# Inverse norms by square root and reciprocal, and another order of work at three places, in a one-core network of three layers

## The reference, cut to what matters

```python
def rms_norm(x, gain):
    y = x * lax.rsqrt(jnp.mean(x * x, axis=-1, keepdims=True) + EPS)
    return y * gain
h = rms_norm(x, norm_mix[i]) * (1.0 + sc1) + sh1
x = x + g1 * mixer(h)
h = rms_norm(x, norm_ffn[i]) * (1.0 + sc2) + sh2
x = x + g2 * conv_ffn(h, ...)
```

## Time and profile before

| what | value |
|---|---|
| median of 3 runs | 1092.78 us (1092.67 to 1094.19) |
| the profiled execution's own time | 1092.73 us |
| its span, first to last instruction | 1091.0 us |
| outside the span | 1.7 us |
| TensorE clock granted, mean | 0.997 |
| busy: TensorE (PE), VectorE (DVE), ScalarE (ACT) | 98%, 74%, 31% |

### The profile page before, as it was taken

How to read it: one execution, slowest core, us unless ns; L and a number is a source line. 1 busy time by engine, 2 the same in 40 slices (tenths; PEclk the granted TensorE clock), 3 DMA queues, 4 the chain that set the end, 5 groups by cost and what they waited for, 6 DMA issues and landing times.

```text
span 1091.0 us, 18364 instructions
## 1 busy us (share of the span) xinstructions
PE 1069.7 (98%) x7516; PEld 972.7 (89%) x7516; DVE 808.4 (74%) x1392; ACT 337.6 (31%) x799; POOL 23.9 (2%) x83
## 2 busy tenths in 40 slices
PE   6999999999999999999999999999999999999998
PEld 4788889999999977888899999998898889999997
DVE  2477769888898848544789889887896298887755
ACT  3243324111111245663511111116355342222101
POOL 1000240000000000000000000000000000000000
PEclk9999999999999999999999999999999999999999
DMA  9999936888878662281868878775342255853421
GB/s 343 281 385 340 316 114 251 304 317 281 320 279 295 199 78 77 86 259 53 318 214 322 313 270 309 271 243 162 117 155 78 80 172 170 290 185 107 145 72 39
DMA packets 163013, 234.82 MB, mean 215 GB/s; under 512 B 8770, under 2 KB 137842, under 8 KB 162930
## 3 DMA queue, kind: packets, MB, share of 16 engines
q1 hardware_dynamic: 162428, 233.27, 63.5%
q10 hardware_dynamic: 501, 0.38, 0.1%
HBM read 232.19 MB, written 1.44 MB: 214 GB/s over the span
## 4 chain that ended last, share of the span: by engine, by line
PE 88%; DVE 7%; ACT 2%; issue 1%; DMA 1%; ACTq 1%; DVEq 0%
PE PS L869 34%; PE PS L915 13%; PE PS L799 11%; PE PS L827 6%; PE PS L990 6%; PE PS L812 4%; PE PS L1117 3%; PE PS L791 1%; PE PS L720 1%; PE PS L1475 1%; DVE scratch L2480 1%; PE PS L1321 1%; PE PS L1277 1%; DVE top L2479 1%; PE PS L1070 1%
## 5 line engine op out<-in xcount | busy, mean ns | idle before, releaser
L915 PE MATMUL PS<-act,slots 128*128 128x256 f32 x704 | 159.8, 380 | 0.4 <-DVE act L2191 0.4
L1962 DVE SCALAR_TENSOR_TENSOR ada_acc<-ada_slots,cond,ada_acc 128x1024 f32<-128x1024 f32 x119 | 152.6, 1282 | 5.1 <-DMA ada_slots<-in_ada_w 0.9
L1607 ACT ACTIVATE PS<-PS 128x128 f32<-128x128 f32 x180 | 53.5, 297 | 304.4 <-PE PS L869 304.4
L915 PEld LDWEIGHTS PS<-act,slots 128*128 128x128 f32 x704 | 130.5, 190 | 18.9 <-issue 1.6
L799 PE MATMUL PS<-hT,slots 128*128 128x256 f32 x656 | 144.3, 380 | 0.8 <-ACT hT L1569 0.8
L799 PEld LDWEIGHTS PS<-hT,slots 128*128 128x128 f32 x656 | 123.9, 190 | 19.2 <-issue 3.0
L869 PE MATMUL PS<-hT,slots 128*128 128x128 f32 x960 | 127.0, 275 | 0.0
L869 PE MATMUL PS<-oT,slots 128*128 128x128 f32 x960 | 126.8, 275 | 0.0
L869 PEld LDWEIGHTS PS<-hT,slots 128*128 128x128 f32 x960 | 119.6, 192 | 2.5
L869 PE MATMUL PS<-oT,scratch 128*128 128x128 f32 x960 | 117.1, 275 | 0.0
L869 PEld LDWEIGHTS PS<-oT,slots 128*128 128x128 f32 x960 | 116.8, 192 | 0.0
(11 more groups left out here) (403 smaller groups left out, 1405.4 us busy)
## 6 DMA issues: line engine op xcount, KB each, us to landing
ada_slots<-in_ada_w SPq DMA_DIRECT2D x144, 512.0 KB, 8.5
slots<-in_ffn_w_up SPq DMA_DIRECT2D x44, 1024.0 KB, 11.8
slots<-in_ffn_w_down SPq DMA_DIRECT2D x22, 1024.0 KB, 5.0
slots<-in_w_up SPq DMA_DIRECT2D x22, 1024.0 KB, 5.2
slots<-in_sb_w_in SPq DMA_DIRECT2D x11, 1024.0 KB, 13.1
slots<-in_w_in SPq DMA_DIRECT2D x11, 1024.0 KB, 5.4
slots<-in_dsa_w_in SPq DMA_DIRECT2D x10, 1024.0 KB, 5.3
ada_slots<-in_w_down SPq DMA_DIRECT2D x2, 2816.0 KB, 12.7
```

What stands on the lines that cost most here:

```text
L915: last = mm(PS[:, c // 2, (c % 2) * T:(c % 2) * T + T], w[:, j_odd * D + c * P:j_odd * D + (c + 1) * P], act[:, j_odd, :], start=start and ...
L1607: act_e.activation(dst.rearrange("p (x t) -> p x t", x=copies), stem(at).unsqueeze(1).to_broadcast([P, copies, P]), ACT.Copy).then_inc(see ...
L1962: ins = dve.scalar_tensor_tensor(dst, ada_slot[k][:, :], c, dst, ALU.mult, ALU.add)
```

## The change

It does four things.

1. Inverse roots. ScalarE's `root` and `norm_root` do one Sqrt (bias epsilon) where they did Ln and Exp, and VectorE does a RECIPROCAL in place behind it: on 128x256 for the six norms and for two of the other roots, on 128x1024 for the recurrence's. `norm_root` preloads the table of Sqrt in place of that of Ln; `norm_raw` preloads that of Silu behind it.
2. Second mixer. TensorE does the index products between and behind the projections of slot 5, and `values(1)` moves from in front of `index(2)` to behind `query_sums(1)`, in front of `turn_sums(1)`. ScalarE's `read_v(1)` goes behind `take_sums(1)`. VectorE's copy of the last projection goes between the second and third pair of heads.
3. Third mixer. `window_norm` stands in front of `decayed_halves(5)`, `decayed_near(6)` behind the two `block_collect`. On ScalarE the first gate stands in front of the second `window_probs`, the second behind the copies of levels 0 and 1; the tables of Silu and Sqrt are preloaded.
4. Last feed-forward stage. `weight_sums` has three parts where it had two halves: only its first sum stands in front of the update of the last chunks.

```diff
 # TensorE, second mixer
-            arrived(5)
-            fill(2)
-            project(4, 5, 0, hT, first_frees=4)
-            project(5, 5, 1, hT).then_inc(unit_full[2], 1)
...
             last.then_inc(unit_full[3], 1)
-            pe.wait_ge(lat_ready, 1)
-            values(0)
+            arrived(5)
+            fill(2)
+            project(4, 5, 0, hT, first_frees=4)
             index(0)
             index(1)
+            project(5, 5, 1, hT).then_inc(unit_full[2], 1)
+            pe.wait_ge(lat_ready, 1)
+            values(0, frees=5)
             pe.wait_ge(k_squared, 1)
             fill(2)
             mm(PS[:, 4, 0:T], ones[:, :], k_sq[:, :], start=True, stop=True).then_inc(unit_full[2], 1)
-            values(1)
             index(2)
             index(3)
...
             scores(0)
             turn_sums(0)
             query_sums(1)
+            values(1)
 # ScalarE
             def root(dst, ps):
                 full(2)
-                link(act_e.activation(dst, ps, ACT.Ln, bias=eps_col[:, :]))
-                act_e.activation(dst, dst, ACT.Exp, scale=-0.5).then_inc(unit_read[2], 1)
-            def norm_root(bank):
-                act_e.preload_act_table(ACT.Ln)
+                act_e.activation(dst, ps, ACT.Sqrt, bias=eps_col[:, :]).then_inc(unit_read[2], 1)
+            def norm_root(bank, load_table=True):
+                if load_table:
+                    act_e.preload_act_table(ACT.Sqrt)
                 act_e.wait_ge(stat_full, bk("stat_full").next())
-                link(act_e.activation(rstd[:, :], PS[:, bank, 0:T], ACT.Ln, bias=eps_col[:, :]))
-                act_e.activation(rstd[:, :], rstd[:, :], ACT.Exp, scale=-0.5).then_inc(rstd_ready, 1)
+                act_e.activation(rstd[:, :], PS[:, bank, 0:T], ACT.Sqrt, bias=eps_col[:, :]).then_inc(norm_root_ready, 1)
 # ScalarE, norm_raw
-                norm_root(0)
+                norm_root(0, load_table)
+                act_e.preload_act_table(ACT.Silu)
 # ScalarE, second mixer
-            read_v(0)
             read_index(0)
             read_index(1)
-            read_v(1)
+            read_v(0)
...
             query_roots(0)
             take_sums(1)
+            read_v(1)
             softmax(0)
 # ScalarE, third mixer
             window_scale()
+            act_e.preload_act_table(ACT.Silu)
+            block_gate(hg, GH0, 0, 0)
             window_probs()
-            block_gate(hg, GH0, 0, 0, 0)
-            block_gate(hg, GH0, 1, 1, 1)
+            skip(0)
+            skip(1)
             full(0)
             act_e.activation(cross, PS[:, 0, :], ACT.Copy).then_inc(unit_read[0], 1)
...
+            block_gate(hg, GH0, 1, 1)
             skip(2)
+            act_e.preload_act_table(ACT.Sqrt)
 # VectorE
+            def inverse_root():
+                dve.wait_ge(norm_root_ready, bk("norm_root_ready").next())
+                link(dve.reciprocal(rstd[:, :], rstd[:, :]))
 # norm() and normalise() call it in place of their wait; in the first norm:
             norm_parts(4)
+            inverse_root()
             dve.wait_ge(ada_used[KC - 1], 1)
...
-            dve.wait_ge(rstd_ready, bk("rstd_ready").next())
 # VectorE, second mixer
-            full(2)
-            dve.tensor_copy(fm[:, 3:5, :], PS[:, 4:6, 0:T]).then_inc(unit_read[2], 1)
...
             for pair in range(IH // 2):
+                if pair == 2:
+                    full(2)
+                    dve.tensor_copy(fm[:, 3:5, :], PS[:, 4:6, 0:T]).then_inc(unit_read[2], 1)
...
                 if n == 4:
                     root()
+                    link(dve.reciprocal(rstd[:, :], rstd[:, :]))
 # VectorE, third mixer
             block_w_sums(GH0 + SLAB, 1)
+            window_norm()
             decayed_halves(5)
-            decayed_near(6)
-            window_norm()
             for i in range(2):
                 block_collect(i, i)
                 dve.nop().then_inc(block_taken, 1)
+            decayed_near(6)
...
             take_scores(4, 1)
             dve.wait_ge(unit_read[2], rstd_taken)
+            link(dve.reciprocal(rstd[:, :], rstd[:, :]))
...
             root()
+            link(dve.reciprocal(sq_flat[:, D:2 * D], sq_flat[:, D:2 * D]))
 # VectorE, weight_sums(l, n, parts=(0, 1, 2)): part 0 is L2076, part 1 L2077, part 2 L2079 and L2080
-                    weight_sums(2, 0, (1,))
+                    weight_sums(2, 0, (1, 2))
```

More of the change, by code:

```diff
@@ L278, in build @@
         stat_full = sem("stat_full")
-        rstd_ready = sem("rstd_ready")
+        norm_root_ready = sem("norm_root_ready")
         gain_ready = sem("gain_ready")
@@ L1213, in _, with values @@
             project(3, 4, 1, hT).then_inc(unit_full[1], 1)
-            arrived(5)
-            fill(2)
-            project(4, 5, 0, hT, first_frees=4)
-            project(5, 5, 1, hT).then_inc(unit_full[2], 1)
-            def values(tt):
+            def values(tt, frees=None):
                 fill(0)
@@ L1223, in values @@
                     last = mm(PS[:, g, :], fm[:, 0, tt * P:(tt + 1) * P], uv_w[:, 8 * g:8 * g + 8, :], start=True, stop=True)
+                    if g == 0 and frees is not None:
+                        last.then_inc(slot_used[frees], 1)
                 last.then_inc(unit_full[0], 1)
@@ L1242, in _ @@
                                     ident[64:64 + IH, 64:64 + IH])
-                if tt == 0:
-                    last.then_inc(slot_used[5], 1)
             last.then_inc(unit_full[3], 1)
-            pe.wait_ge(lat_ready, 1)
-            values(0)
+            arrived(5)
+            fill(2)
+            project(4, 5, 0, hT, first_frees=4)
             index(0)
             index(1)
+            project(5, 5, 1, hT).then_inc(unit_full[2], 1)
+            pe.wait_ge(lat_ready, 1)
+            values(0, frees=5)
             pe.wait_ge(k_squared, 1)
@@ L1573, in squares, with norm_raw @@
                 act_e.activation(hT[:, c:c + k, :], xT[:, c:c + k, :], ACT.Square, scale=D ** -0.5).then_inc(sq_ready, 1)
-            def norm_raw(units):
+            def norm_raw(units, load_table=True):
                 act_e.wait_ge(gain_ready, bk("gain_ready").next())
@@ L1834, in window_scale, with block_gate @@
                     last.then_inc(p_ready, 1)
-            def block_gate(dst, name_at, u, i, buf):
-                skip(u)
+            def block_gate(dst, name_at, i, buf):
                 act_e.wait_ge(block_taken, i + 1)
@@ L1902, in _ @@
             root(sq_flat[:, D:2 * D].rearrange("p (b n) -> p b n", b=2), PS[:, 4:6, :])
-            norm_raw(OUT_UNITS[2])
+            norm_raw(OUT_UNITS[2], load_table=False)
             ffn(2)
@@ L2063, in out_projection, with weight_sums @@
                         after()
-            def weight_sums(l, n, halves=(0, 1)):
+            def weight_sums(l, n, parts=(0, 1, 2)):
                 g, v = LAST_SETS[(n + 1) % 3] if l == 2 else (3 - 3 * (n % 2), 4 - 3 * (n % 2))
                 gate, val, ws = slot[g], slot[v], w_sum[n % 2]
-                if 0 in halves:
+                if 0 in parts:
                     for s, landed in zip((g, v), up_landed[l, n + 1]):
@@ L2076, in weight_sums @@
                     link(dve.tensor_tensor(ws[:, 0, :, :], val[:, 0:HALF, :], val[:, HALF:KC, :], ALU.add))
+                if 1 in parts:
                     link(dve.tensor_tensor(val[:, 0:HALF, :], gate[:, 0:HALF, :], val[:, 0:HALF, :], ALU.subtract))
-                if 1 in halves:
+                if 2 in parts:
                     link(dve.tensor_tensor(ws[:, 1, :, :], ws[:, 0, :, :], gate[:, 0:HALF, :], ALU.subtract))
@@ L2237, in last_chunks @@
                         if not odd and n + 1 < 10:
-                            weight_sums(2, n + 1, (1,))
+                            weight_sums(2, n + 1, (2,))
                         elif odd and n + 2 < 10:
-                            weight_sums(2, n + 2, (0,))
+                            weight_sums(2, n + 2, (0, 1))
                         elif p == 17:
@@ L2300, in ffn @@
                         chunk(odd, odd, raw[:, odd, 0, :], raw[:, odd, 1, :])
-                    weight_sums(2, 1, (0,))
+                    weight_sums(2, 1, (0, 1))
                     for odd in range(2):
```

## The result

After the change the kernel takes 1100.79 us (median of 4 runs, 1100.01 to 1103.92); beside it the kernel before took 1092.72. The ratio is 1.0077 (95% interval 1.0064 to 1.0089): 8.1 us slower, where the prediction had +2.95 and a range that ended at 1099.5. The profiled execution took 1100.2, with a span of 1098.5 and a mean granted clock of 0.998.

The account below looks back on a forecast made before the run. TensorE, busy 98% of the span, was taken to bound the kernel, so only holes closing or opening count. Stalls behind reciprocals less the reorderings' gains summed to +2.95 us on 1092.73, 1095.7; the 8-in-10 range was 1088.6 to 1099.5.

Parts of the forecast that it names:

- The term of the reciprocal: VectorE's reciprocal priced at 4.8 ns an element: 1.39 us on 128x256 and 5.1 us on 128x1024.
- the first norm: First norm: the reciprocal runs ahead of the conditioning vector's sums, so TensorE starts later, +0.9 us.
- the two feed-forward stages: Norms before the first and second feed-forward stage: the reciprocal outlasts VectorE's 0.6 us of slack, +0.8 us each.
- attention: Attention's root, third mixer: the reciprocal exceeds VectorE's 0.2 us of slack, +1.2 us.
- the recurrence: Recurrence's root: the 128x1024 reciprocal delays `mixed_ready` to 862.8, past TensorE's cover until 860.3, +2.5 us.
- third rival: All the new reciprocals: 8.3 ns an element, 2.3 and 8.7 us, about 1105 us in total; chance 0.07.
- the likeliest case: Whole kernel: reciprocal at the slope of its two small sizes, range 1094 to 1100.6 us; chance 0.56.
- Second mixer: Second mixer's new order: earlier index products close holes, a new one of 0.9 to 1.2 opens at `read_v(1)`; -0.25 us.
- Third mixer: Third mixer's new order: load and first gates ahead of the second `window_probs` close TensorE's 1.7 and 0.26 us holes; -1.9 us.
- Rival 2: Hole at `read_v(1)` or late gates do not pay, 1.9 us gain shrinks to 1: 1096.7; chance within the likeliest's 0.56.
- Rival 1: All new reciprocals as fast as other VectorE work, 0.43 and 1.23 us: 1089.1 us, faster; chance 0.27.
- Rival 4: ScalarE's roots: the table load stays because another function comes between preload and Sqrt, costing 1.3 us at two norms; chance 0.02.

Follow-up runs that it names:

- experiment 6: The kernel before with six unused reciprocals on 4 to 512 elements, one behind the other, in VectorE's second mixer: 1094.46 us, a single run.
- experiment 5: The kernel after, with TensorE making 9 products that nobody reads while it waits for `mixed_ready`: 1099.15 us, ratio 1.0058 to the kernel before.
- experiment 2: The kernel before with all inverse roots by Sqrt and reciprocal, the orders as they were: 1108.53 us, ratio 1.0138.
- experiment 12: The kernel before, no order changed, with the table set holding both Ln and Exp preloaded by name and Silu's behind: 1091.41 us, ratio 0.9986.
- experiment 7: The kernel before with only the second mixer's new order, roots by Ln and Exp: 1092.55 us, ratio 0.9999 to the kernel before.
- experiments 9: The kernel after with Ln and Exp back, their shared table set preloaded by name and Silu's behind the Exp: 1087.30 us, ratio 0.9951 to the kernel before.

## Why the prediction was wrong

**The direction and the places were right, the size was not.** The stalls behind the reciprocals, the new hole at `read_v(1)`, no wait of L1472: all stand in the trace where the steps had them. Three things failed: the price of the reciprocal, the clock behind a stall, which the sum put at nothing, and the upper end of the range.

*The term of the reciprocal.* "I take the slope of its own two rows": 4.8 ns an element, measured 6.25 (experiment 6), so 1.75 us for 1.39 and 6.55 for 5.1. Put into the same steps, with no other change: the first norm 1.26 (measured 1.26); the two feed-forward stages 1.15 each (measured 1.35, 1.27); the mixers' norms +0.05 each (measured +0.06, +0.05); attention 1.55 (1.65); the recurrence 864.3 - 860.3 = 4.0 (4.1). The sum becomes 1.26 + 2.3 + 0.1 + 1.55 + 4.0 - 0.25 - 1.9 - 0.5 = +6.6 us, 1099.3. Of the 5.1 us that the forecast was short, 3.6 are this one number. The slack that I read for each place from the starts of before was right to 0.2 us. The trace of before had a warning that I read wrongly: TENSOR_TENSOR does not keep the 1.2 ns an element of its two small sizes up to large tiles. From 159 ns at one element to 1.23 us at 1024 it is 1.05, so two such sizes had already missed the slope of another instruction. The Trainium skill (VectorE: DVE Perf Modes, the fixed hardware budget) has the repeat count of 8 that spoke for the third rival. It gives no time; eight cycles an element, my reading of it, would be an estimated 8.3 ns, and the trace's 6.25 doesn't agree.

*The clock behind a stall.* The sum took each idle us of TensorE at its face. It had looked at the granted clock only for the first norm. Behind the 4.1 us at the recurrence's root TensorE ran at 1.2 GHz for 3.4 us and lost 1.8 (experiment 5: 1.7). With it the sum is +8.4, the measured one 8.1. That they agree to 0.3 is in part luck: the 8.1 holds a start that varies by more, and behind 42 us the corrected steps give 7.1 where the ledger has 7.7. The longest stall that I forecast was 2.5 us; whether it would bring a slow clock no run says, but the trace of before had a reason to ask: TensorE waits 3.7 and 1.9 us for its first data, up to 12.1 us, and from 13.0 us its clock is 0.51 for 3.5 us. In the mixers waits of 2.7 and 3.9 us were followed by the lower clock (experiment 2), those of 1.1 to 1.8 us weren't; in the start two of 1.4 and 1.2 us close together once were (experiment 12).

*The range.* The upper end of my own bounds gave 1100.6, and the likeliest case's own range ended there, but the range put on record ended at 1099.5. The dearest price of the likeliest case (6.8 us, measured 6.55) was in the working and was then left out to bring the range to 8 in 10. Even 1100.6 is 0.2 short of the measured 1100.8, since the clock is not in it. The narrowing should have been at the fast end: the slope spoke against the lower price, and it got 0.27.

**Point by point, the rest.** Second mixer: -0.25 forecast, -0.2 by itself (experiment 7), and the new hole, 0.9 to 1.2, is 1.26. The text had both terms, the loop's earlier start and what the reciprocal gives back, but not what this means for the parts: the order pays for the reciprocal, and without it the loop over the best keys, which "ends earlier anyway", ends 1.8 us late and `turn(0)` waits for it (experiment 2). Third mixer: -1.9 forecast, -2.0 measured, by the mechanism described. Less the 2.65 us by which the kernel is late there, `window_scale` ends at 822.8, the load at 824.1 and the gates at 825.0, where I had 823.1, 824.4 and 825.4. Rival 2's wait doesn't come about: the exponentials end at 821.7 and VectorE, which has worked on without a break, takes them up at 822.2; ScalarE stands idle for 0.88 us in front of L1833, which costs TensorE nothing. Last stage: -0.5 forecast, -0.78 at its start, and -0.63 with the two small ones. Rival 1 (a fast reciprocal) and rival 3 (8.3 ns) fell with experiment 6. Rival 4: the loads between the root's two functions are gone, as the change says.

**The root on ScalarE.** I took the loads at the Exp's line for given because the trace showed six of them. By the Trainium skill (ScalarE: Activation LUTs, table sets) there is a set that holds both Ln and Exp. Both were right: with the table preloaded by function (`ACT.Ln`) the trace has a load at each Exp that follows a Ln, and with the shared set named it has none there (experiments 9 and 12). The root was cheap on ScalarE after all; what was dear was one load of 1.28 us, and that could be saved without a single instruction on VectorE.

## What to carry to other kernels

Price an operation at the size at which it will run: two sizes of a few elements give the fixed part and no slope, and where nothing larger is in the trace the range must reach as far as its dearest reading. In a kernel whose TensorE is busy 98% of the time, ask before moving work off ScalarE whether the costly part is the work or a table load between two functions that one set could hold. And judge a new order with the edits that it stands beside: the same one was worth nothing alone and 3.3 us next to a reciprocal (the mixer cost 3.4 us without the new order and 0.1 with it).

## What the runs showed of the hardware

- RECIPROCAL on VectorE takes 153 ns and 6.25 ns for each element of a partition in float32, on a straight line from 4 to 1024 elements; at 1024 it is 5.3 times a TENSOR_TENSOR (6.55 against 1.23 us).
- Idle waits of TensorE of 2.7 and 3.9 us were followed by stretches at a granted clock of 0.52 to 0.54, 3.4 us long twice and 6.8 us once, in which matmuls come at half the rate. Filling the wait with products of no use kept the clock at 1.00 and gained 1.7 us. Waits of 1.1 to 1.8 us in the mixers and feed-forward stages were not followed by one; two of 1.4 and 1.2 us close together near 38 us were in one kernel and not in others.
- With the table preloaded by function, ScalarE has a load of 1.28 us where Exp follows Ln or Ln Exp: six at the norms' Exp, three at that of the other roots, eight in the first layer's attention. With the set that holds both preloaded by its name there are none of these (1092.85 to 1091.41 us by itself).
- The first 42 us of a profile vary by some 3 us between kernels that are alike there, and some vary by 0.3 to 0.4 once more, near 68 us. Part of it is a 3.5 us stretch at half clock, at 13 us or at 39 us; part is that the first matmuls come at half rate for a differing time, which the clock in the profile's rows doesn't show (1.00 where 40 products took 4.50 us instead of 2.37). Two profiles are compared behind this, not from 0.
